# Hybrid SSD/attention/MoE step on one core: expert weight loads issued behind the landing of the unit two places ahead

## Chip, cores and metric

One NeuronCore of a Trainium2 chip, fp32 inputs and outputs. The metric is the device time of one execution in microseconds; lower is better. The median of 3 runs of the kernel before is 777.38 us.

## The reference, cut to what matters

Two layers over 384 tokens of width 1024 (128 context tokens and 256 latent tokens). Each layer has an adaLN-modulated RMSNorm, an attention and state-space mixer, a gated residual, a second modulated norm and a mixture of experts (MoE). The change touches only how the weights of the MoE arrive. What it computes:

```
scores = sigmoid(t @ w_router)                    # 384 tokens x 16 experts
best group of 4 experts per token, then the top 2 experts in it; gates from their scores
hid = silu(t @ w_gate[e]) * (t @ w_up[e]) * gate  # w_gate, w_up: 1024 x 256 per expert
out = sum over e of hid @ w_down[e]               # w_down: 256 x 1024 per expert
```

All 16 experts of both layers are used, so every expert's 3.1 MB is read from HBM once per layer.

## The kernel before, in words

**Units.** All large weights arrive in units of 2 MiB (2.10 MB), each made of two DMAs of 1024 KB, issued by SP. `ORDER` lists the 84 units u = 0 to 83 in the order of issue: those of the conditioning, the input projection, the output projection and, from `MOE_AT[l]` = 22 and 60 on, 24 MoE units per layer. A MoE unit is either the gate and up weights of one expert (k = 0 or 1 of a pair) or the down weights of a pair of experts (k = 2). In this document "place j" is MoE unit j of a layer, j = 0 to 23.

**Slots.** A ring in SBUF has six slots (`SLOTS`), and within the MoE two more lie over an arena that is then free (`EXTRAS`). `SLOT[u]` is the slot of a unit and `EARLIER[u]` the unit that held it; SP waits in L585 until PE has made the last product with that one (`used`, on `s_gu` or `s_dn`). Places 6 and 7 are the first ones in the two extra slots; they have no earlier holder and wait instead for the hidden state to be updated and stored (L587 to L592).

**Landing.** A DMA adds 16 to `landed[u % LANDED]`, eight semaphores in turn, so unit u has landed when its semaphore reaches 32 * (u // 8 + 1). PE waits for exactly this before its first product with a unit (L1804, `arrived`). SP itself waits for no landing of a weight.

**Order of the loads.** Experts are numbered by how many tokens chose them. Experts 0 to 2 are fixed; the others are known only when DVE has ranked them, so SP waits in L580 for `s_order` before place 5 and reads each later expert's number from a register. Place 4 (`SPLIT`) holds the down weights of experts 2 and 3: the half of expert 2 is issued in its place, the half of expert 3 only behind place 5, when expert 3 is known. Behind the MoE loads of layer 0, SP waits for the gathered results (L603) before it issues the input weights of layer 1.

**Blocks.** The tokens of the experts are packed into ten blocks (`BLOCKS`) of 128 rows. For block b, PE makes the gate and up products (L2329, from `gate_up`), ACT and DVE make the hidden rows, PE turns them (L2336), turns the gathered rows of block b + 2 (L2320) and makes the down products of block b (L2344). Place 21 is the gate and up unit of the last expert (its loads go into the arena) and serves the last block, block 9; places 22 and 23 are the last down units.

**The other queues.** POOL gathers the rows of blocks 1 to 9 from HBM (L797, 512 KB each) and, at the end of the MoE, the results of every token (L804, six of 512 KB). ACT stores the results of blocks 0 to 6 to HBM (L1089, 512 KB per block); those of the last three blocks stay in SBUF, and PE adds them by products with a selection (L2390). Every load of a weight is issued in `load` (L534) on SP's queue, q1 in the profile; q0 is POOL's and q10 is ACT's.

Of the kernel before, what the change touches and what calls it, by code (L numbers as in the profile page):

```python
# [40 lines left out]
SLOTS, EXTRAS, LANDED = 6, (6, 7), 8  # L41
# [12 lines left out]
IN_AT, OUT_AT, MOE_AT = [], [], []  # L54
# [137 lines left out]
def hybrid_step(nc, x_prompt, x_sample, cache_k, cache_v, state_ssm, c, c_ctx, norm1_w, norm2_w,  # L192
# [9 lines left out]
    with ctx:  # L202
# [3 lines left out]
        def sem(name):  # L206
            return ctx.enter_context(nc.semaphore(name))
# [157 lines left out]
        landed = [sem(f"landed{i}") for i in range(LANDED)]  # L365
# [58 lines left out]
        def slot(u):  # L424
            return ring[:, SLOT[u], :].rearrange("p (k n) -> p k n", k=KT)

        def unit_at(s):

            return extras[EXTRAS.index(s)] if s in EXTRAS else ring[:, s, :]
# [65 lines left out]
        def overflow(eng, l, step, start=None, stop=None, end=None, more=None):  # L495

            if more is None:
                more = rounds_of(eng, l)
            before = done_rounds.get((id(eng), l - 1), 0)
            with eng.If(more > 0):  # L500
                with eng.Fori(0, more) as r:
                    if start:
                        start(before + r)
                    with eng.Fori(0, E) as e:
                        step(e, before * E + r * E + e)
                    if stop:
                        stop(before + r)
                if end:
                    end(before * E + more * E)
            done_rounds[id(eng), l] = before + more  # L510
# [4 lines left out]
        @block.sync  # L515
        def _(sp):
            def used(u):

                kind, n = ORDER[u]
                if kind == "ada":  # L520
                    return s_ada, n + 1
                if kind == "in":
                    l, j = divmod(n, IN_U)
                    return ((s_q, NT * (l + 1)), (s_xbc, XM * l + 2), (s_xbc, XM * (l + 1)), (s_z, NT * (l + 1)))[j]
                if kind == "out":
                    l, j = divmod(n, OUT_U)
                    return s_o, 2 * NT * l + 5 + j
                l, j = divmod(n, MOE_U)
                pair, k = MOE_UNITS[j]
                return (s_gu, NB * l + GU_BLOCK[2 * pair + k] + 1) if k < 2 else (s_dn, NB * l + DN_BLOCK[pair] + 1)  # L530

            def load(s, parts):
                for dst, src in parts:
                    sp.dma_start(dst, src).then_inc(landed[s], 16)  # L534

            def columns(u, w):
                v = w.rearrange("(k p) n -> p k n", p=P)
                if EARLIER[u] is not None:
                    sp.wait_ge(*used(EARLIER[u]))
                load(u % LANDED, [(slot(u)[:, 4 * i:4 * i + 4, :], v[:, 4 * i:4 * i + 4, :]) for i in range(2)])  # L540

            def ada_unit(u, n):

                l, c = n // ADA_U, ADA_COL[n] % ADA_U
                columns(u, w_ada[l, :, c * 512:(c + 1) * 512])

            def following(u):
                kind, n = ORDER[u]
                if kind == "ada":
                    return ada_unit(u, n)  # L550
                w, units = {"in": (w_in, IN_U), "out": (w_out, OUT_U)}[kind]
                columns(u, w[n // units, :, n % units * 512:(n % units + 1) * 512])

            def gate_up_unit(l, e, u):

                load(u % LANDED, [(unit_at(SLOT[u])[:, i * KT * F:(i + 1) * KT * F], by_row(w[l, e]))
                                  for i, w in enumerate((w_gate, w_up))])

            def down_half(l, e, i, u):

                load(u % LANDED, [(unit_at(SLOT[u])[:, i * 2 * DM:(i + 1) * 2 * DM],
                                   w_down[l, e].rearrange("(p f) n -> p (f n)", f=2))])


            for dst, src in ((prm_rows[32:40, :], c_ctx.rearrange("(k p) -> k p", p=P)),
                             (prm_rows[40:48, :], rows(c)),
                             (prm_rows[108:120, :], rows(conv_b))):
                sp.dma_start(dst, src).then_inc(s_rows, 16)
            u = 0
            for l in range(DEPTH):  # L570
                while u < MOE_AT[l]:
                    if u == 0:
                        sp.dma_start(x[:, 0, :], x_prompt[0]).then_inc(s_x, 16)
                        sp.dma_start(x[:, 1:3, :], x_sample[0].rearrange("(t p) d -> p t d", p=P)).then_inc(s_x, 16)
                    following(u)
                    u += 1
                expert = {x: x for x in range(FIXED)}
                for pair, k in MOE_UNITS:
                    if (pair, k) == (SPLIT[0], 1):
                        sp.wait_ge(s_order, l + 1)  # L580
                    if k < 2 and RANK_OF[2 * pair + k] is not None:
                        r = RANK_OF[2 * pair + k]
                        expert[2 * pair + k] = sp.value_load(order[0:1, r:r + 1], min_val=FIXED, max_val=E - 1)
                    if EARLIER[u] is not None:
                        sp.wait_ge(*used(EARLIER[u]))  # L585
                    else:
                        sp.wait_ge(s_x1, 2 * NT * (l + 1))  # L587
                        if SLOT[u] == EXTRAS[0]:
                            sp.wait_ge(s_bt, 6 * (l + 1))
                        else:  # L590
                            sp.wait_ge(s_h, 16 * NT * (l + 1))
                            sp.wait_ge(s_tx, NB * l + 1)  # L592
                    if k < 2:
                        gate_up_unit(l, expert[2 * pair + k], u)
                    else:
                        for i in range(1 if (pair, k) == SPLIT else 2):
                            down_half(l, expert[2 * pair + i], i, u)
                    if (pair, k) == (SPLIT[0], 1):
                        down_half(l, expert[2 * pair + 1], 1, MOE_AT[l] + UNIT_AT[SPLIT])
                    u += 1  # L600
                if l + 1 < DEPTH:

                    sp.wait_ge(combined[NT - 1], 32 * (l + 1))  # L603
                    while u <= IN_AT[l + 1][-1]:
                        following(u)
                        u += 1

                sp.wait_ge(s_dn, NB * (l + 1))

                def again(e, q):  # L610
                    sp.wait_ge(o_dn, q + 1)
                    for i, w in enumerate((w_gate, w_up)):
                        sp.dma_start(ring[:, OVER_GU, i * KT * F:(i + 1) * KT * F], by_row(w[l, e])
                                     ).then_inc(o_w, 16)
                    sp.dma_start(ring[:, OVER_DN, 0:2 * DM],
                                 w_down[l, e].rearrange("(p f) n -> p (f n)", f=2)).then_inc(o_w, 16)

                def all_used(steps):
                    sp.wait_ge(o_dn, steps + 1)
                    sp.sem_inc(o_pass, 1)  # L620

                overflow(sp, l, again, end=all_used)
            for t in range(NT):
                sp.wait_ge(s_y_out, t + 1)
                dst = y_prompt[0] if t == 0 else y_sample[0, (t - 1) * P:t * P, :]
                sp.dma_start(dst, xn[:, t, :]).then_inc(s_yst, 16)
            sp.wait_ge(s_yst, 16 * NT)
            sp.wait_ge(s_out, 16 * STORES * DEPTH)
# [1854 lines left out]
```

## Time and profile before

| | us |
|---|---|
| median of 3 runs | 777.38 |
| lowest and highest run | 775.66, 777.53 |
| the profiled execution, its own time | 776.23 |
| its span (first to last instruction) | 774.5 |
| PE busy | 724.9 (94%) |
| DVE busy | 324.9 (42%) |
| ACT busy | 213.1 (28%) |
| POOL busy | 138.2 (18%) |
| moved by DMA | 209.33 MB, mean 270 GB/s |
| of it on SP's queue | 179.33 MB |

All times below are microseconds from the start of the span. PE is TensorE, DVE is VectorE, ACT is ScalarE, POOL is GpSimd, SP is SyncE. A name with q behind it (SPq) is the engine's issuing of DMAs. The chain of waits is followed back from the last instruction to what released each piece of work. A row of the timeline or the chain gives start, duration and what ran; a bracket gives the idle time before it and what ended it. PEclk is the granted TensorE clock as a share of 2.4 GHz. The MoE of layer 0 lies at about 250 to 385 us, that of layer 1 at about 618 to 765 us.

### The profile page before, as it was taken

The page shows a single profiled execution, that of the slowest core. Times are in us where ns is not written, and L with a number is a line of the kernel's source. Part 1 is how long each engine was busy: PE and PEld are TensorE (multiplying, and loading weights), DVE is VectorE, ACT ScalarE, POOL GpSimd, SP SyncE. Part 2 cuts the span into 40 slices and gives each one's busy share as a digit, 9 for nine tenths or more (in the row PEclk, how much of TensorE's full clock was granted, in tenths as well). Part 3 has the DMA queues.
Part 4 walks back from the last instruction along what each step waited for, and adds up shares of the span by engine and source line. Part 5 has one row for each costly group of instructions (what it writes and reads, how often), then busy time and mean ns, then how long its engine had stood idle before and what let it go on. Part 6 is the DMA issues. An engine that isn't in the chain of part 4 may idle for free.

```text
span 774.5 us, 10382 instructions
## 1 busy us (share of the span) xinstructions
PE 724.9 (94%) x3940; PEld 354.9 (46%) x3940; DVE 324.9 (42%) x877; ACT 213.1 (28%) x486; POOL 138.2 (18%) x232
## 2 busy tenths in 40 slices
PE   3999998999999999998999999889999899999994
PEld 1447553446445534433344755334544653443331
DVE  2022625637635553312362252473763555231137
ACT  2220145845024101011212024574502310110131
POOL 4056032220010101101112503322001011010202
PEclk9999999999999999999999999999999999999998
DMA  8997335989309899999896233578720389999962
GB/s 319 387 355 263 110 115 212 331 315 364 110 3 337 325 382 391 423 421 423 311 388 230 98 108 116 178 258 306 264 110 4 133 324 390 412 422 423 421 246 82
DMA packets 65639, 209.33 MB, mean 270 GB/s; under 512 B 7736, under 2 KB 8608, under 8 KB 53299
## 3 DMA queue, kind: packets, MB, share of 16 engines
q1 hardware_dynamic: 52744, 179.33, 60.2%
q10 hardware_dynamic: 7723, 16.65, 5.7%
q0 software_dynamic: 5120, 12.66, 4.5%
q8 instruction: 32, 0.52, 0.3%
q14 instruction: 20, 0.16, 0.1%
HBM read 199.92 MB, written 12.88 MB: 275 GB/s over the span
## 4 chain that ended last, share of the span: by engine, by line
PE 75%; DMA 9%; DVE 5%; ACT 4%; SPq 3%; issue 2%; POOL 1%; ACTq 1%; POOLq 0%; DVEq 0%
PE bank L2329 14%; PE bank L2213 11%; PE bank L1955 8%; PE bank L2344 7%; PE bank L2012 5%; PE bank L1900 4%; PE bank L1824 4%; DMA arena<-in_w_up_dram 3%; PE bank L1941 3%; SPq L534 2%; PE bank L2390 2%; DMA ring<-in_w_ada_dram 2%; PE bank L2320 2%; PE bank L2057 2%; DMA arena<-y_exp,y_idx 2%
## 5 line engine op out<-in xcount | busy, mean ns | idle before, releaser
L2329 PE MATMUL bank<-ring,work 128*32 128x512 f32 (+1 forms) x640 | 116.0, 597 | 4.4 <-DMA arena<-in_w_up_dram 3.7
L2329 PEld LDWEIGHTS bank<-ring,work 128*32 128x32 f32 (+1 forms) x640 | 33.7, 121 | 78.1 <-issue 75.0
L2344 PE MATMUL bank<-ring,xs_tok 128*64 128x512 f32 (+2 forms) x320 | 65.7, 597 | 1.5 <-DVE xs_tok L1665 1.0
L1665 DVE COPY xs_tok<-bank 128x256 f32<-128x256 f32 x20 | 8.5, 425 | 138.3 <-PE bank L2336 138.3
L1955 PE MATMUL bank<-arena,ring 128*128 128x384 f32 x192 | 62.2, 486 | 0.0
L2329 PE MATMUL bank<-arena,work 128*64 128x512 f32 (+1 forms) x128 | 58.6, 612 | 0.0
L1824 PE MATMUL bank<-ring,cpad 128*32 128x512 f32 x384 | 50.8, 621 | 7.2 <-DMA ring<-in_w_ada_dram 5.7
L797 POOL DMA_INDIRECT gather_at<-h_rows,idx x18 | 18.2, 1011 | 176.6 <-PE bank L2320 121.2
L1955 PEld LDWEIGHTS bank<-arena,ring 128*128 128x128 f32 x192 | 36.5, 190 | 25.0
L1076 ACT ACTIVATE xs_tok<-bank 128x256 f32<-128x256 f32 x20 | 7.7, 384 | 132.0 <-PE bank L2329 132.0
L2213 PE MATMUL bank<-ring,arena 128*128 128x512 f32 x96 | 43.6, 597 | 0.0
L2213 PE MATMUL bank<-ring,xs_tok 128*128 128x512 f32 x96 | 43.2, 592 | 0.0
L1900 PE MATMUL bank<-ring,arena 128*128 128x512 f32 x96 | 42.8, 597 | 0.4 <-ACT arena L887 0.4
L2012 PE MATMUL bank<-ring,arena 128*128 128x512 f32 x96 | 42.3, 593 | 0.0
L1083 ACT ACTIVATE qkv<-bank 128x512 f32<-128x512 f32 x36 | 19.5, 595 | 74.6 <-PE bank L2344 74.6
L2344 PEld LDWEIGHTS bank<-ring,xs_tok 128*64 128x64 f32 (+2 forms) x320 | 20.5, 131 | 35.0 <-issue 31.4
L1548 DVE COPY work<-bank 128x512 f32<-128x512 f32 x38 | 24.6, 687 | 18.2 <-PE bank L2320 14.5
L1256 DVE SCALAR_TENSOR_TENSOR conv<-arena,prm,conv 128x388 f32<-128x388 f32 x48 | 29.9, 623 | 1.7
L1305 DVE CUSTOM_DVE_ANT_0 arena<-bank,amask 128x384 f32<-128x384 f32 (+1 forms) x48 | 20.1, 466 | 23.9 <-PE bank L2029 23.6
L2213 PEld LDWEIGHTS bank<-ring,xs_tok 128*128 128x128 f32 x96 | 18.2, 190 | 23.0 <-issue 23.0
L2329 PEld LDWEIGHTS bank<-arena,work 128*64 128x64 f32 (+1 forms) x128 | 20.6, 166 | 16.7 <-issue 16.7
L1900 PEld LDWEIGHTS bank<-ring,arena 128*128 128x128 f32 x96 | 17.7, 190 | 22.6 <-issue 20.4
(381 smaller groups left out, 1085.6 us busy)
## 6 DMA issues: line engine op xcount, KB each, us to landing
ring<-in_w_ada_dram SPq DMA_DIRECT2D x48, 1024.0 KB
ring<-in_w_down_dram SPq DMA_DIRECT2D x28, 1024.0 KB
ring<-in_w_gate_dram SPq DMA_DIRECT2D x24, 1024.0 KB
ring<-in_w_up_dram SPq DMA_DIRECT2D x24, 1024.0 KB
ring<-in_w_in_dram SPq DMA_DIRECT2D x16, 1024.0 KB
ring<-in_w_out_dram SPq DMA_DIRECT2D x8, 1024.0 KB
arena<-in_w_gate_dram SPq DMA_DIRECT2D x8, 1024.0 KB
arena<-in_w_up_dram SPq DMA_DIRECT2D x8, 1024.0 KB
```

Of the source, the lines that this page charges most:

```text
L1083: act.activation(y_buf(e)[:, hf * 512:(hf + 1) * 512], bank[5 + hf][:, :], ACT.Copy).then_inc(s_yc, 1)
L1256: ins = dve.scalar_tensor_tensor(out=conv[:, m, :], in0=xpd[:, m, k:k + CONVW], scalar=tap(k), in1=conv[:, m, :], op0=ALU.mult, op1=ALU.add)
L1305: dve.tensor_tensor_reduce(out=probs(t, h), in0=bank[SCORE_BANK[i // 2 % 2][i % 2]][:, 0:nk], in1=amask[:, m0:m0 + nk // P, :].rearrange(" ...
L1548: dve.tensor_copy(xgT[:, b, hf * 512:(hf + 1) * 512], bank[3 + hf][:, :]).then_inc(s_xgc, 1)
L1824: last = mm(bank_of(i)[ADA_TILE * q:ADA_TILE * (q + 1), :], cpad[:, c:c + ADA_TILE], slot(ADA_AT[j])[:, kt, :], start=j == a and kt < ADA_ ...
L1900: last = mm(bank[t][:, :], tok(kt, t), slot(u[0])[:, kt, :], start=kt == 0, stop=kt == KT - 1)
L1941: last = mm(bank[3 + t][:, 0:256], tok(kt, t), slot(u[1])[:, kt, 0:256], start=kt == 0, stop=kt == KT - 1)
L1955: last = mm(bank[(6 + m) % 8][:, 0:3 * P], slot(v)[:, kt, col:col + P], hT[:, kt, :], start=kt == 0, stop=kt == KT - 1)
L2012: last = mm(bank[4 + t][:, :], tok(kt, t), slot(u[3])[:, kt, :], start=kt == 0, stop=kt == KT - 1)
L2213: last = mm(bank[2 * t + hf][:, :], mixed[:, t, kt * P:(kt + 1) * P] if kt < 4 else xs_tok[:, t, (kt - 4) * P:(kt - 3) * P], slot(u + hf)[ ...
L2329: last = mm(bank[b][at:at + n, :].rearrange("p (i f) -> p i f", i=2), rows_T[:, kt * P + at:kt * P + at + n], gate_up_of(s)[:, kt, :, :], ...
L2344: last = mm(bank[5 + hf][at:at + n, :], hidT[:, b, f * P + at:f * P + at + n], w[:, f, hf * 512:(hf + 1) * 512], start=f == 0, stop=f == 1)
```

## The change

Before the DMAs of a MoE unit at place 6 or later are issued, SP now also waits until the unit two places ahead of it has landed. The wait stands behind the wait for the slot. Places 0 to 5, and the units outside the MoE, are issued as before.

```diff
@@ def load(s, parts) ... @@
                 for dst, src in parts:
                     sp.dma_start(dst, src).then_inc(landed[s], 16)
 
+            def landed_first(u):
+
+                sp.wait_ge(landed[u % LANDED], 32 * (u // LANDED + 1))
+
             def columns(u, w):
...
                             sp.wait_ge(s_h, 16 * NT * (l + 1))
                             sp.wait_ge(s_tx, NB * l + 1)
+                    if u >= MOE_AT[l] + SLOTS:
+                        landed_first(u - 2)
                     if k < 2:
                         gate_up_unit(l, expert[2 * pair + k], u)
                     else:
```

## Rows read from the trace of the kernel before

**Rows 1.** The page's 40 slices of 19.4 us: GB/s moved

```profile
GB/s 319 387 355 263 110 115 212 331 315 364 110 3 337 325 382 391 423 421 423 311 388 230 98 108 116 178 258 306 264 110 4 133 324 390 412 422 423 421 246 82
```

**Rows 2.** Windows; from:to, length, five engines' busy us, PEclk, DMA share, GB/s

```profile
287.00:291.00 4.00, 4.00 (x34) 1.80 (x28) 2.14 (x8) 0.38 (x1) 0.00 (x0) 1.00 0.69 229
320.00:330.00 10.00, 10.00 (x80) 4.26 (x74) 4.72 (x17) 0.96 (x3) 0.99 (x1) 1.00 1.02 424
367.02:371.30 4.28, 4.28 (x12) 1.56 (x14) 0.00 (x0) 0.00 (x0) 2.97 (x3) 0.60 1.00 410
653.00:658.00 5.00, 5.00 (x42) 2.13 (x36) 3.10 (x11) 0.38 (x1) 0.69 (x1) 1.00 0.89 317
732.40:737.00 4.60, 4.59 (x22) 1.93 (x24) 0.00 (x0) 0.00 (x0) 3.38 (x5) 1.00 1.01 417
```

**Rows 3.** The chain of waits: start, us, what

```profile
256.91 10.25 DMA gather_at<-h_rows,idx
...
341.85 25.03 DMA arena<-in_w_up_dram
...
367.02 8.78 PE bank L2329 x32
...
707.48 7.02 PE bank L2329 x32
...
736.71 12.85 DMA arena<-y_exp,y_idx
```

**Rows 4.** The timeline of PE, the last row of DVE

```profile
267.21 1.09 PE L2320 MATMUL bank<-ident,gather_at 128*128 128x128 f32 x8 [0.47 <-DMA gather_at<-h_rows,idx]
...
367.02 0.61 PE L2329 MATMUL bank<-ring,work 128*64 128x512 f32 x1 [2.26 <-DMA arena<-in_w_up_dram]
...
732.41 0.61 PE L2329 MATMUL bank<-ring,work 128*64 128x512 f32 x1 [1.40 <-DMA arena<-in_w_up_dram]
...
745.77 3.65 PE L2344 MATMUL bank<-ring,xs_tok 128*64 128x512 f32 x16 [0.50 <-DMA ring<-in_w_down_dram]
...
762.33 1.88 PE L2390 MATMUL bank<-work,qT 128*128 128x512 f32 x4
...
765.11 1.28 DVE L1757 TENSOR_TENSOR arena<-bank,conv 128x512 f32<-128x512 f32 x2
```

**Rows 5.** Who waited for whom, PE: us in total, times, longest

```profile
PE bank L2329 <- DMA arena<-in_w_up_dram: 3.7, 2, 2.3
```

**Rows 6.** SP's DMA queue from 341 to 367 us: packets, MB, share

```profile
q1 hardware_dynamic: 1288, 9.38, 86.1%
```

**Rows 7.** The timeline of SP's issues

```profile
255.15 0.36 SPq L534 DMA_DIRECT2D ring<-in_w_gate_dram  x1
...
257.30 0.34 SPq L534 DMA_DIRECT2D arena<-in_w_gate_dram  x1
...
289.18 0.33 SPq L534 DMA_DIRECT2D ring<-in_w_gate_dram  x1
...
341.42 0.33 SPq L534 DMA_DIRECT2D arena<-in_w_gate_dram  x1
...
622.48 0.34 SPq L534 DMA_DIRECT2D ring<-in_w_gate_dram  x1
```

**Rows 8.** Transfers of 231.3:235.3, 255:268 and 622:635, the latter in 40 slices

```profile
DMA packets 126, 1.03 MB, mean 258 GB/s; under 512 B 0, under 2 KB 0, under 8 KB 0
...
GB/s 0 0 0 202 101 151 302 403 403 403 403 403 403 429 454 429 403 429 429 416 404 416 466 454 378 391 441 429 429 429 429 378 403 454 429 378 403 429 429 454
...
GB/s 0 0 0 50 202 0 176 252 479 403 403 403 429 429 403 403 429 403 429 429 429 479 353 466 429 378 479 441 454 366 416 441 391 454 403 403 429 403 403 429
```

**Rows 9.** SP's DMA queue from 742 to 743 and 745 to 745.8 us

```profile
q1 hardware_dynamic: 18, 0.13, 31.5%
...
q1 hardware_dynamic: 1, 0.00, 0.1%
```

**Rows 10.** POOL's gathers of rows (L797) in layer 0

```profile
DMA to landing us min/median/max: 9.0/9.1/9.6
```

## The prediction, made before the changed kernel was built or run

> **What bounds the kernel now.** I read the 40 slices first, to see where TensorE and the DMA engines are full together. A slice is 19.4 us. In the slices from 290 to 368 us and from 639 to 736 us the transfers run at 390 to 423 GB/s, and no slice of the kernel is above 423 [rows 1]. These are the two mixture-of-experts stages. A window inside one shows PE busy 10.00 of 10.00 us and the DMA share at 1.02, at 424 GB/s [rows 2]. So in this stage a transfer slot that is lost is lost, unless a dry stretch comes later that can take it up.
>
> The chain of waits shows what ends the stage. In layer 0 the last step from a transfer into PE is the load of place 21, the last gate and up weights: its second half is issued at 341.85 us and lands 25.03 us later. The block behind it takes 8.78 us where the same 32 products take 7.02 us in a block that was not held up [rows 3]. The timeline of PE gives the pauses themselves: 2.26 us before 367.02 and 1.40 us before 732.41, both for place 21 of its layer, and 0.50 us before 745.77 for the last down weights; the products of one block wait for a gate and up load nowhere else (3.7 us, 2 times in all) [rows 4, 5]. The windows give the clock's part: after the pause in layer 0 the granted clock is 0.60 in the mean over 4.28 us, so part of it at 1.2 GHz; behind the shorter one in layer 1 it stays at 1.00, 2.4 GHz [rows 2]. So weight landings set PE at the end of both stages, and everything before that has cover.
>
> **The change, part by part.** It adds 36 waits on SP, 18 per layer, from place 6 on: unit u is issued only when u-2 has landed. No byte, load or product is added, and nothing runs on another engine. Queued behind a waiting SP are only the other weight loads; gathers go out from POOL, result stores from ACT. Behind the MoE loads of layer 0 stand the input weights of layer 1, which wait for the gathered results anyway.
>
> *A wait that is already fulfilled.* It is one more small step of a queue whose issues last 0.3 to 0.4 us each, with long pauses between them [rows 7]; I cost it at nothing. The cover is the weights already in flight; with the queue empty a wait would cost its own length, far below 0.3 us.
>
> *The steady stretch.* Between 341 and 367 us SP's queue moved 9.38 MB in 26 us, 361 GB/s [rows 6]. A unit is 2.10 MB, hence 5.8 us. The load issued at 341.42 [rows 7] landed at 366.88, 25.5 us later, so it had more than three units ahead of it. Under the change it is issued when the unit two ahead has landed, 366.88 - 2 x 5.8 = 355.3 us: 14 us later, yet still one unit (5.8 us) ahead of its turn. What a start needs is the time from issue to flow. I take it from three starts into an empty queue [rows 8]. From 231.3 to 235.3 us 1.03 MB moved where 424 GB/s would have moved 1.70: 0.67 MB short, 1.6 us. In the eight slices of 0.325 us from 255.0 the rates add to 1159 where full ones would add to 3392, short by 1.7 us, 0.15 of it before the issue at 255.15 [rows 7]; the same sum from 622.0 (680) is short by 2.1 us, 0.5 us of which lies before the issue at 622.48 [rows 7]. So 1.6 us. Behind it comes the lag from the last bytes to the landing: the last down weights release PE at 745.77, and from 745.0 on their queue moved nothing [rows 4, 9]: 0.8 us. The two together, 2.4 us, are less than 5.8. In the steady stretch the cost is 0; the upper end is below, as a rival.
>
> *The first wait, at place 6.* Place 4 is the split one: its first half goes out early, its second half after place 5, once the order of the experts is known. So "two places ahead" is here the last thing in the queue: loads at 255.15 and behind them that half, and today right after it place 6 at 257.30 [rows 7]. With the change this one waits until the queue is empty: three halves of 1.05 MB and two gathers of 0.52 MB, 4.2 MB at 424 GB/s, are 9.9 us, so to about 255.15 + 1.6 + 9.9 = 266.7 us. It costs 1.6 + 0.8 = 2.4 us of transfer time in each layer. Unevenness of the 16 engines adds to it: at 742 to 743 us the queue is already down to a share of 31.5% while it drains, so some engines run out some 2 to 3 us before the last [rows 9]. An engine idle on the average for 1 us more makes 3.4 us; the low end is 1.6 us, the start alone. I take 2.4.
>
> *What takes it up.* PE doesn't need place 6 soon (it serves block 3, and the only pauses for gate and up weights are those before block 9 [rows 4, 5]), so the loss counts only as a later stream. The stream of before runs dry once more, because a slot comes free late (the load issued at 289.18 [rows 7]): 287 to 291 us at 229 of 424 GB/s is a gap of 4 x (1 - 0.54) = 1.8 us; in layer 1, 653 to 658 us at 317 GB/s is 1.3 us [rows 2]. A delay up to there closes that gap. Net: layer 0 2.4 - 1.8 = 0.6 us (ends 0 and 1.6), layer 1 2.4 - 1.3 = 1.1 us (ends 0.3 and 2.1).
>
> *What a later stream costs.* Layer 0: place 21 lands 0.6 us later and PE, already waiting for it, starts 0.6 us later; the half clock is paid now as before. The chain from there on is PE's: +0.6 us. Layer 1: the pause grows from 1.40 to 2.5 us, more than the 2.26 us that came before the half clock in layer 0. I add that loss, 8.78 - 7.02 = 1.76 us [rows 3], to PE: +1.1 + 1.8 = +2.9, less the 0.50 us it now waits for the last weights: +2.4. At the end DVE takes up some of it: PE's last products end at 764.21 and DVE starts on them at 765.11 [rows 4], 0.9 us of slack. But the last gathered results (736.71 + 12.85 us in the chain [rows 3]) share the same full engines and shift by about 1.1. The larger of 2.4 - 0.9 = 1.5 and 1.1 counts: +1.5 us. The ends are 0.3 (no half clock) and 3.2 us.
>
> *A gain.* At 267.16 the first gather ends and PE had waited 0.47 us for it [rows 3, 4]; with place 6 held back, SP's queue thins out behind it. At most -0.5 us; I take -0.1, since the 3 MB issued before are still ahead.
>
> *Longer waits in passing.* The blocks in the middle never waited for weights [rows 5]. Still, I put +0.6 us for the 34 other waits together (a few starts that come a few tenths late): low 0, high 5.
>
> **Sum:** 0.6 + 1.5 - 0.1 + 0.6 = +2.6 us. The profiled execution took 776.23 us (span 774.5, 1.7 around it): 778.8. The median of the runs lies 1.15 us above the profiled one: 780.0.
>
> The Trainium skill, "DMA: Bandwidth & Descriptors", section "Anatomy of one DMA", gives a fixed cost of about 2.0 us for setup and completion of a transfer on GpSimd's path. By it, an estimate from that page, the bubble would be 2.0 instead of 2.4 us and the sum 0.8 us less. The rows above are of SP's own queue, so they decide.
>
> **The rivals.**
> (A) *It makes nothing.* The bubble is swallowed by the dry stretch and nothing else moves: -1 to +1.5 us. For it: in layer 0 the dry stretch is nearly as large. Against it: in layer 1 it is half. 778.
>
> (B) *Faster: engines in step, shorter queues.* If the 424 GB/s is one shared limit and not sixteen, holding the leading engines back hands their share to the last one, whose landing releases PE. The lead is some 2 to 3 us [rows 9], so a landing comes 1 to 1.5 us earlier; in layer 0 the pause falls to 1 us, at which layer 1 kept its clock: 1.2 + 1.8, and about 1 us in layer 1, less bubbles of 1.7: about -2.3, 775. Against it: the gathers take 9.0 to 9.6 us under full load, all within 0.6 us of each other [rows 10], which looks like a fixed price and not like a queue that stands behind SP's.
> The Trainium skill, same page, section "Queues, rings and completion order", says that each DMA engine goes round-robin over the queue rows with work. By that rule the depth of SP's queue is nothing to the others. The spread of the gathers agrees with it.
>
> (C) *Slower by more: the steady stretch starves.* At a landing only 5.8 us of weights are left, less on a leading engine. The margin is 5.8 - 2.4 = 3.4 us; from where an engine leads by more, it stands idle each time. If the leads are due to chance and move from engine to engine, the loss isn't made good. At 0.4 us for each of about 12 units per layer it is 5 us of stream, per layer, all on the path from place 21: with the above +10, 787. For it: leads of 2 to 3 us are near 3.4.
>
> (D) *The waits hold nothing back*, since slots come free later than u-2 lands. Against it: the load issued at 341.42 landed 25.5 us later. It would give 777.4, and counts with (A).
>
> **How the numbers follow.** Chances: forecast 0.50 (+1.3 to +5 us), A with D 0.25, B 0.13, C 0.12. A measurement of this kernel can tell about 0.3%, 2.3 us, from no change. Of the forecast 0.34 lies above that and 0.16 below; C is slower; a tenth of B stays within. Slower 0.46, same 0.43, faster 0.11. The range runs from 776 (all but B's better half) to 784, 0.8% above the median; what is left out is C's larger part and B's.
>
> **What would show it.** Right: place 6 issued at about 267 in layer 0 and, by the same sum from 622.48, at about 634 in layer 1, with a hole of 2 to 3 us in the DMA slices there; the hole before 291 closed; the pause before block 9 in layer 0 at 2.5 to 3.5 us; a clock below 1.00 after the one in layer 1; the issue of place 21 near 356 us instead of 341.4; DMA share at 1.01 still. Wrong: place 21 of layer 0 landing before 366.9; a share below 0.98 in the steady stretch (C); gathers that land in under 8 us (B).

## The result and the profile after

| | before | changed |
|---|---|---|
| median, us | 777.38 | 783.98 |
| lowest and highest of 7 runs | 775.66, 777.53 | 782.53, 788.22 |
| the profiled execution, its own time | 776.23 | 788.22 |
| its span | 774.5 | 786.5 |
| ratio to before, 95% interval | | 1.0100 (1.0084 to 1.0115) |

The change makes the kernel slower: the medians differ by 6.6 us (0.8%), and the ratio, which is not simply that of the two medians, gives 1.0%, 7.8 us. A second measurement, against other runs of before, gave 1.0108 (1.0092 to 1.0124), 8.4 us. The forecast was slower by 2.6 us, at 780.0; the median, 783.98, lies just inside the edge of the stated range, but the rise is 2.5 to 3 times the forecast one.

The profiled execution is the slowest of the seven, so its steps are sized against its own +12.0 us of span; a second profile of the same kernel follows below. First the page's 40 slices of the changed kernel:

```profile
PEclk9999999999999999999999999999999999999898
DMA  8996336998217799999895233678531289999951
GB/s 320 387 356 241 108 113 226 343 326 311 107 63 286 305 393 399 409 414 421 337 386 184 79 107 114 213 243 321 214 108 53 82 343 403 400 414 416 409 213 80
```

Where the fullest slices of before held 421 to 423 GB/s in both MoE stages [rows 1], there are now 399 to 421 and 400 to 416. The windows of the changed kernel (from:to, length, five engines' busy us, PEclk, DMA share, GB/s) show where it begins, and what came after the pauses:

```profile
255.00:273.00 18.00, 17.12 (x145) 8.90 (x146) 8.62 (x29) 2.26 (x3) 3.17 (x3) 1.00 0.74 284
273.00:303.00 30.00, 30.00 (x200) 12.01 (x200) 12.72 (x61) 3.33 (x7) 1.98 (x2) 1.00 0.99 388
303.00:357.00 54.00, 52.40 (x304) 20.52 (x298) 14.18 (x43) 6.96 (x14) 3.96 (x4) 1.00 1.01 413
...
371.94:378.00 6.06, 6.06 (x18) 2.08 (x20) 0.00 (x0) 0.00 (x0) 0.00 (x0) 0.61 1.01 414
...
742.85:749.00 6.15, 6.15 (x16) 2.04 (x18) 0.00 (x0) 0.00 (x0) 1.85 (x2) 0.52 1.02 422
```

The same three stretches of the kernel before, for comparison:

```profile
255.00:273.00 18.00, 17.15 (x144) 8.80 (x144) 8.43 (x29) 2.26 (x3) 3.17 (x3) 1.00 0.95 381
273.00:303.00 30.00, 30.00 (x200) 12.03 (x200) 12.93 (x61) 3.33 (x7) 2.18 (x3) 1.00 0.96 375
303.00:357.00 54.00, 54.00 (x310) 21.04 (x304) 13.96 (x43) 6.96 (x14) 3.75 (x4) 1.00 1.02 423
```

Against before, the first stretch lost 18 x (381 - 284) = 1.75 MB, 4.1 us at 424 GB/s. The second won back 30 x (388 - 375) = 0.39 MB, 0.9 us, and the third lost 54 x (423 - 413) = 0.54 MB, 1.3 us. So there are two losses: a hole at the start and a slightly thinner steady stretch. The dry stretch from 287 to 291 us did close, as forecast: 408 GB/s there instead of 229.

The hole of layer 1 is smaller. The same 18 us, laid from 0.15 us before the issue of place 5, in the kernel before and in the changed one:

```profile
622.33:640.33 18.00, 17.61 (x144) 8.48 (x144) 8.21 (x24) 2.26 (x3) 3.16 (x3) 1.00 0.94 380
...
628.06:646.06 18.00, 17.55 (x142) 8.44 (x142) 8.22 (x24) 2.26 (x3) 3.16 (x3) 1.00 0.82 311
```

That is 18 x (380 - 311) = 1.24 MB, 2.9 us.

Inside the hole of layer 0, the slices of 0.2 us from 262 to 270 us of the changed kernel:

```profile
GB/s 512 307 533 389 430 410 471 328 512 492 246 451 328 82 246 82 0 0 0 0 0 0 0 0 1 164 164 143 225 307 205 82 225 143 41 143 410 287 287 369
```

The timeline of SP's issues (compare [rows 7]):

```profile
256.27 0.38 SPq L534 DMA_DIRECT2D ring<-in_w_down_dram  x1
267.46 0.34 SPq L534 DMA_DIRECT2D arena<-in_w_gate_dram  x1
268.32 0.34 SPq L534 DMA_DIRECT2D arena<-in_w_up_dram  x1
...
360.54 0.33 SPq L534 DMA_DIRECT2D arena<-in_w_gate_dram  x1
...
639.28 0.33 SPq L534 DMA_DIRECT2D arena<-in_w_gate_dram  x1
```

Place 6 goes out at 267.46 us instead of 257.30. The rates are full until 264.4, at zero from 265.2 to 266.8, and full again only from 269.2. Between the last bytes and SP's next issue lie 2.2 us (the landing itself comes at 267.22), and 1.7 us more between that issue and full flow. What moves from 267.0 us on, before SP's issue, is a gather of POOL.

In layer 1 the same wait ended sooner. The slices of 0.1 us from 637 to 641 us of the changed kernel:

```profile
GB/s 615 164 328 328 246 328 410 328 123 205 164 41 164 41 82 41 0 0 0 0 0 0 1 0 246 246 123 41 205 123 369 328 451 287 164 205 123 164 123 41
```

The rates thin out from 637.8, the last bytes move before 638.6, and place 6 goes out at 639.28: 0.7 us. Every traced kernel in which place 6 waits for place 4 shows this difference (the change, e1, e3, e4, e5, e9, e10 and e12): from the last bytes of SP's own queue to the issue about 2.5 us in layer 0 and about 0.9 us in layer 1. Why layer 0 waits longer, no run shows.

The end of the stage, in the chain of waits of the changed kernel (start, us, what), to be read beside [rows 3]:

```profile
360.97 10.84 DMA arena<-in_w_up_dram
...
371.94 9.44 PE bank L2335 x32
...
742.85 10.01 PE bank L2335 x32
```

And the pauses, in the timeline of PE:

```profile
354.88 7.09 PE L2335 MATMUL bank<-ring,work 128*64 128x512 f32 x32 [1.60 <-DMA ring<-in_w_up_dram]
...
371.94 1.09 PE L2335 MATMUL bank<-ring,work 128*64 128x512 f32 x1 [5.14 <-DMA arena<-in_w_up_dram]
...
725.95 7.09 PE L2335 MATMUL bank<-ring,work 128*64 128x512 f32 x32 [0.82 <-DMA ring<-in_w_up_dram]
...
742.85 1.09 PE L2335 MATMUL bank<-ring,work 128*64 128x512 f32 x1 [4.99 <-DMA arena<-in_w_up_dram]
```

Layer 0: the pause before block 9 grew from 2.26 to 5.14 us, one of 1.60 before block 8 is new, and the block itself took 9.44 us instead of 8.78: +5.1 us. Layer 1: 1.40 became 4.99, 0.82 is new, the block took 10.01 instead of 7.0, and the pause of 0.50 for the last down weights is gone: +6.9 us, of which DVE at the end takes up some. By the order of the experts (628.21 instead of 622.48 us at place 5) the shift was 5.7 us; at the end it is 12.0. PE's other work is untouched.

The bytes until the landing of place 21 show one thing more. POOL issues its gathers of the results at about 364 us in either kernel. In the kernel before none of their bytes had moved when place 21 landed at 366.88; in the changed kernel its queue moved this between 357 and 371.8 us:

```profile
q0 software_dynamic: 220, 0.61, 10.6%
```

So a late place 21 shares the engines with them. From 255 us on, 1.75 - 0.39 + 0.54 = 1.90 MB of transfers were lost (4.5 us), these 0.61 MB went ahead (1.4 us), and SP's queue had moved 37.39 instead of 37.86 MB by the landing, 0.47 MB less of the weights behind place 21 (-1.1 us): 4.8 of the 4.9 us by which the block starts later (371.94 against 367.02).

### The profile page after: what moved, and what is told of

It is laid out like the page before. It is cut to its first block, busy times and chain, and to the rows that moved or that the text cites. A ratio compares the mean times of both kernels' runs of the same rounds, so it can differ in the third digit from the quotient of the medians.

```text
span 786.5 us, 10416 instructions
## 1 busy us (share of the span) xinstructions
PE 728.4 (93%) x3940; PEld 355.4 (45%) x3940; DVE 325.2 (41%) x877; ACT 212.8 (27%) x486; POOL 135.9 (17%) x232
## 4 chain that ended last, share of the span: by engine, by line
PE 55%; DMA 29%; DVE 5%; SPq 4%; ACT 3%; issue 2%; ACTq 1%; POOL 0%; POOLq 0%; DVEq 0%
PE bank L2219 11%; DMA arena<-in_w_up_dram 9%; DMA ring<-in_w_up_dram 9%; PE bank L1961 8%; PE bank L2018 5%; DMA ring<-in_w_down_dram 5%; PE bank L1906 4%; PE bank L1830 4%; PE bank L2396 4%; SPq L534 4%; DMA arena<-in_w_down_dram 3%; PE bank L1947 3%; PE bank L2335 2%; DMA ring<-in_w_ada_dram 2%; PE bank L2350 2%
## 5 line engine op out<-in xcount | busy, mean ns | idle before, releaser
L2335 PE MATMUL bank<-ring,work 128*32 128x512 f32 (+1 forms) x640 | 119.8, 604 | 13.3 <-DMA arena<-in_w_up_dram 10.1
L2335 PEld LDWEIGHTS bank<-ring,work 128*32 128x32 f32 (+1 forms) x640 | 35.3, 122 | 89.9 <-issue 86.8
L2335 PE MATMUL bank<-arena,work 128*64 128x512 f32 (+1 forms) x128 | 62.1, 642 | 0.0
```

The costliest lines, as they stand in the source:

```text
L2335: last = mm(bank[b][at:at + n, :].rearrange("p (i f) -> p i f", i=2), rows_T[:, kt * P + at:kt * P + at + n], gate_up_of(s)[:, kt, :, :], ...
```

## The experiments

All medians stand against runs of the kernel before on the same chip, in groups: 776.40 us for e1 to e4, 776.12 for e5 to e8, 776.21 for e9 to e11 and 776.13 for e12 and e13. A cost in us below is the ratio less 1, times that median.

### e1, e2: the first wait alone, the others alone

```diff
-                    if u >= MOE_AT[l] + SLOTS:
+                    if u == MOE_AT[l] + SLOTS:     # e1; e2: if u > MOE_AT[l] + SLOTS:
                         landed_first(u - 2)
```

> The only wait left is that of place 6, behind the landing of place 4 (whose second half is the last load in the queue). First theory (the emptied queue at place 6 is the cause): some 3.5 to 4 us of transfers are lost in each layer, 1.6 us of it is taken up at 287 to 291 us in layer 0 and 0.7 us in layer 1; with the longer pauses of PE and the half clock behind them this gives +4 to +5 us of the +6.6, and place 21 of layer 0 lands 2 to 3 us later than in the kernel before. Second theory (the many waits of the steady stretch are the cause): under +2 us, place 21 within 1 us of the kernel before.

> All waits of the change but that of place 6, so the queue never runs empty at place 6. First theory: +1 to +2.5 us, what the steady stretch lost in the trace (1.3 us of transfers between 303 and 357 us in layer 0, about as much in layer 1), with the DMA share at 1.01 and 416 to 424 GB/s there. Second theory: +4 to +6 us. If the sum of this and of the kernel with place 6 alone is well above 6.6 us, the two hide behind each other; if it is well below, they need each other.

e1: 781.67 us, ratio 1.0063 (1.0049 to 1.0077), +4.9 us. e2: 777.03 us, 1.0010 (0.9998 to 1.0022), +0.8 us. One wait per layer makes most of the loss, the other 34 almost none by themselves. The sum, 5.7 us, is less than the whole (7.8 and 8.4 us in the two measurements of the change). The windows of e1:

```profile
255.00:273.00 18.00, 17.20 (x144) 8.81 (x144) 8.44 (x29) 2.27 (x3) 3.17 (x3) 1.00 0.77 283
273.00:303.00 30.00, 30.00 (x200) 12.03 (x200) 12.97 (x61) 3.33 (x7) 2.24 (x3) 1.00 1.01 414
303.00:357.00 54.00, 53.56 (x308) 21.00 (x302) 13.91 (x43) 6.97 (x14) 3.71 (x4) 1.00 1.02 422
```

The hole is the same as in the change (283 GB/s). But behind it the queue is full without a gap, at 414 GB/s, and wins back 30 x (414 - 375) = 1.2 MB, and the steady stretch is back at 422. What the waits at the later places add is to be seen beside the second profile of the change, below.

### e3: the change once more

> The change itself once more. Its profiled execution took 788.22 us, while the other six took 782.5 to 785.0. Theory of the clock: the difference between executions is how much half clock falls behind the two pauses; this profile should again show pauses before block 9 of about 5 us in both layers, and a total of 783 to 785 us where the half clock is shorter. Rival: the transfers differ from execution to execution, then the landing of place 21 moves by some us against the start of its stage.

784.58 us (781.84 to 786.45). Its profiled execution took 781.84 us, the fastest of its five. The timeline of PE there:

```profile
369.29 1.08 PE L2335 MATMUL bank<-ring,work 128*64 128x512 f32 x1 [4.67 <-DMA arena<-in_w_up_dram]
...
737.67 0.61 PE L2335 MATMUL bank<-ring,work 128*64 128x512 f32 x1 [3.58 <-DMA arena<-in_w_up_dram]
```

The chain of waits gives the two blocks:

```profile
369.29 9.22 PE bank L2335 x32
...
737.67 8.78 PE bank L2335 x32
```

Pause and landing move too: place 21 starts PE at 369.29 instead of 371.94 us, with no pause before block 8 in either layer. So both the rival and the theory have a part: of the 6.4 us between the two profiled executions 4.3 us are pauses and 1.5 us are the two blocks (9.22 and 8.78 us against 9.44 and 10.01). The transfers of one and the same kernel differ by some 2.5 us at place 21 between executions. The windows of this execution:

```profile
273.00:303.00 30.00, 30.00 (x204) 11.99 (x204) 13.16 (x62) 3.33 (x7) 2.42 (x3) 1.00 1.01 412
303.00:357.00 54.00, 54.00 (x310) 21.23 (x304) 13.72 (x43) 6.97 (x14) 3.53 (x4) 1.00 1.01 413
```

Behind the same hole (287 GB/s from 255 to 273 us) this execution wins back 30 x (412 - 375) = 1.1 MB, 2.6 us, as e1 does. The 0.9 us of the first profile is therefore no rule of the change. What both executions share is the thinner steady stretch: 413 GB/s, where e1 has 422 and the kernel before 423.

### e4, e5, e6: PE's clock kept

Small products of PE into a free bank are put ahead of the wait for block 9: 16 and 8 of them in the change (e4, e5), 3 in the kernel before (e6).

```diff
                 for b in range(NB):
+                    if b + 1 == NB - 1:
+                        clock_kept(2, 8)     # e4: 16; e6: 3, in the kernel before
                     if b + 1 < NB:
```

> The change, with 16 small products of PE ahead of its wait for block 9, some 3.9 us inside the pause of 5 us, so that PE's clock has no reason to fall; transfers untouched. Theory of the clock (the half clock behind the pauses is a part of the loss): block 9's gate and up products take 7.0 us instead of 9.4 and 10.0, and the time falls by 2 to 4 us against the change, to 780 to 782. Rival (the pauses alone cost, the clock is taken up later): within 1 us of the change.

> The change with 8 small products of PE ahead of block 9's wait. Sixteen of them ran 7.1 us (0.44 us each) and were longer than the pause of 4.7 to 5.1 us; eight run 3.6 us and lie inside it. Theory of the clock: block 9's gate and up products take 7.0 us instead of 8.8 to 10.0 in both layers and the time falls by 2 to 3.5 us against the change. Rival: what the clock costs is taken up behind block 9 (by the wait for the last down weights, by DVE at the end), and it stays within 1 us of the change.

> The kernel before with 3 such products, 1.3 us, ahead of block 9's wait, inside its pauses of 2.3 and 1.4 us; no waits added. Theory of the clock: the idle time left is 1 us, the half clock of 3.4 us in layer 0 goes, block 9 takes 7.0 us instead of 8.8: -1 to -1.8 us. But the last down weights of layer 0 landed only 1.1 us before PE came to them, so 0.7 us of it may turn into a pause for them. Rival: the half clock does not fall in most executions, then no change (within 0.5 us).

e4: 786.08 us, 1.0118 (1.0100 to 1.0136). It answers another question than the one I asked, since I had sized the filler wrongly. Its timeline of PE:

```profile
366.27 7.17 PE L1858 MATMUL bank<-amask,ident 128*128 128x256 f32 x32
373.38 0.64 PE L2335 MATMUL bank<-ring,work 128*64 128x512 f32 x1
```

Sixteen ran for 7.17 us, longer than the pause, and PE came late by itself. But block 9 took the 7.02 us of a block that was not held up, in both layers, so the filler does keep the clock; in the chain of waits of e4:

```profile
373.44 7.02 PE bank L2335 x32
...
745.32 7.02 PE bank L2335 x32
```

e5: 782.66 us, 1.0072 (1.0051 to 1.0093), +5.6 us. Against the 1.0108 of the change without the filler that is 2.8 us less, as the theory had it, though the two intervals just overlap, and by the medians, each against its own runs of before (+6.5 and +8.2 us), it is only 1.6 us. In e5 another wait comes up, for the last down weights:

```profile
383.07 3.65 PE L2350 MATMUL bank<-ring,xs_tok 128*64 128x512 f32 x16 [1.85 <-DMA ring<-in_w_down_dram]
...
752.37 5.35 PE L2350 MATMUL bank<-ring,xs_tok 128*64 128x512 f32 x16 [2.28 <-DMA ring<-in_w_down_dram]
```

The second of these took 5.35 us for the 16 products that take 3.65 us in the first: behind the pause of 2.28 us the half clock falls here instead, as the granted clock of that stretch (0.68) shows:

```profile
752.37:757.70 5.33, 5.33 (x17) 1.78 (x17) 3.56 (x3) 2.29 (x2) 0.00 (x0) 0.68 0.05 20
```

So a part of what the clock gives back is taken by the next late load. e6: 775.82 us, 0.9997 (0.9985 to 1.0009): in the kernel before the filler gains nothing that can be measured. No version here beats the kernel before.

### e8, e11: the same place, but the queue not emptied

```diff
-                    if u >= MOE_AT[l] + SLOTS:
-                        landed_first(u - 2)
+                    if u == MOE_AT[l] + SLOTS:      # e8: this wait alone
+                        landed_first(u - 1)
+                    if u >= MOE_AT[l] + SLOTS:      # e11: all 36, place 6 behind place 5
+                        landed_first(u - (1 if u == MOE_AT[l] + SLOTS else 2))
```

> One wait per layer only, that of place 6, but behind the landing of place 5 instead of place 4. Behind place 5 the second half of place 4 (1.05 MB) is still in the queue, 2.5 to 4 us of transfers. First theory (it is the emptied queue that costs, not a wait at this place): the hole shrinks to 0 to 1.5 us, which the dry stretch behind it takes up: within 1 us of the kernel before. Rival (holding back the loads at this place costs by itself, whatever is in flight): +3 to +5 us, as with the wait for place 4.

> All 36 waits of the change, but place 6 waits for the landing of place 5 instead of place 4, so that one half load is still in flight. If the emptied queue is what both parts need: within 0.3% of the kernel before, +0 to +1.5 us. Rival (any delay at place 6 takes away the cover of the later waits): +2.5 to +4 us.

e8: 776.24 us, 0.9995 (0.9983 to 1.0007), no cost that can be measured. Its place 6 was issued at 263.05 us, also held back, but with half a unit still in flight:

```profile
255.00:273.00 18.00, 16.66 (x142) 8.77 (x142) 8.34 (x29) 2.26 (x3) 3.17 (x3) 1.00 0.91 359
273.00:303.00 30.00, 30.00 (x196) 12.06 (x196) 12.50 (x62) 3.33 (x7) 1.98 (x2) 1.00 0.97 381
```

The first stretch has 359 GB/s where the change had 284. e11, with all 36 waits, one of them moved by one place: 777.56 us, 1.0016 (1.0003 to 1.0029), +1.2 us instead of +8.4. It is the emptied queue that costs, not that SP waits. (Its place 6 went out at 262.68 us, some 5 us earlier than in the change; a delay as long as that of the change with the queue still full was not tried.)

### e7: the price of a start, many times

```diff
                     if u >= MOE_AT[l] + SLOTS:
-                        landed_first(u - 2)
+                        landed_first(u - 1)
```

> The suspected cost made many: from place 6 on each unit waits for the landing of the unit directly before it, so nearly each of 18 units per layer starts into an empty queue. First theory: each such start costs 3 to 4 us of transfers (2 us from the last bytes to the landing, 1.5 to 2 us from the issue to full flow), so a unit takes some 9 to 10 us instead of 6, and the stream of a layer gets 45 to 65 us longer: +90 to +130 us in all. Rival (a start costs 2.4 us, as I put it in the prediction): +55 to +75 us.

864.54 us, 1.1133 (1.1103 to 1.1162), +87.9 us: below the 90 of the first theory, above the 75 of the rival. SP's issues there give the price:

```profile
365.41 0.33 SPq L534 DMA_DIRECT2D ring<-in_w_gate_dram  x1
...
372.81 0.33 SPq L534 DMA_DIRECT2D ring<-in_w_gate_dram  x1
...
381.32 0.81 SPq L534 DMA_DIRECT2D ring<-in_w_down_dram  x2
388.71 0.33 SPq L534 DMA_DIRECT2D ring<-in_w_gate_dram  x1
...
396.09 0.33 SPq L534 DMA_DIRECT2D arena<-in_w_gate_dram  x1
```

Three of these units took 7.4 us from issue to issue; 2.10 MB at 424 GB/s are 4.95, so a start out of an empty queue costs 2.4 us. In two of the three, from 365.41 and from 381.32 us, no other queue moved anything. The end of the latter, from 386 to 390 us in slices of 0.1 us:

```profile
GB/s 328 410 573 328 328 573 410 328 492 492 164 573 573 164 573 573 164 410 164 0 0 0 0 0 0 0 0 0 0 0 0 0 0 0 0 0 246 246 164 0
```

The last bytes move before 387.9, the next issue comes at 388.71: 0.8 us, and 0.7 and 0.9 us at the issues of 381.32 and 372.81. That is the price of the prediction, in its lag of 0.8 us too. The hole at place 6 is larger than a clean start, by 0.5 us in layer 1 and by 1.7 us in layer 0.

### e9, e10: which waits add to the first

```diff
-                    if u >= MOE_AT[l] + SLOTS:
+                    if MOE_AT[l] + SLOTS <= u < MOE_AT[l] + 12:                    # e9
+                    if u == MOE_AT[l] + SLOTS or u >= MOE_AT[l] + 12:              # e10
```

> Place 6 alone cost 4.9 us, the other waits alone 0.8 us, all together 8.2 us against the same runs of before: the rest needs both. First theory (the dry stretches at 287 to 291 and 653 to 658 us can hide one loss only: alone, the waits of places 7 to 11 are hidden there, but behind the hole of place 6 they are not): waits at places 6 to 11 give nearly the full +7 to +8 us. Second theory (with a late stream the limit of two units in flight binds in the steady stretch, at places 12 to 23): +5 us, as with place 6 alone.

> Waits at place 6 and at places 12 to 23, none at 7 to 11. First theory (one dry stretch, two losses before it): +5 to +5.8 us, place 6 plus at most the 0.8 us of the rest. Second theory (the limit binds in the steady stretch once the stream is late): +7 to +8 us, with 400 to 415 GB/s between 303 and 357 us instead of 421 to 424.

e9: 783.27 us, 1.0092 (1.0078 to 1.0106). e10: 783.30 us, 1.0093 (1.0078 to 1.0109). Both cost some +7.2 us. Each theory foretold its own kernel and missed the other's, so neither holds alone: on top of place 6 (+4.9) either half of the other waits adds about 2.2 us, and both halves together little more (+7.8 to +8.4 in the two measurements of the change). The windows of layer 0, one execution each, fit: from 273 to 303 us e9 has 396 GB/s and e10 417, from 303 to 357 us e9 has 422 and e10 414, where e1 has 414 and 422.

### e12, e13: do the costs add once the clock is kept?

```diff
                 for b in range(NB):
+                    if b + 1 == NB - 1:
+                        clock_kept(2, 8)     # e12: in e1; e13: clock_kept(2, 4) in e2
                     if b + 1 < NB:
```

> The wait of place 6 alone, with 8 small products of PE (3.6 us) in the pause before block 9, which was 4.7 and 3.6 us. Theory: the clock makes the costs more than additive, since a half clock follows only behind a longer pause. Then with the clock kept, place 6 alone costs +2.5 to +4 us instead of +4.9, and this plus the cost of the other waits with the clock kept (the next kernel) is within 1.5 us of the +5.6 that the whole change costs with the clock kept. Rival (the transfers themselves need both): place 6 alone with the clock kept +1 to +2.5 us, the other waits +0.5, and the sum stays 2.5 us or more below 5.6.

> All waits but that of place 6, with 4 small products (1.8 us) in the pause before block 9, which was 2.1 and 3.3 us. Theory of the clock: +0.5 to +2 us, as without them (+0.8) or a little less, since a half clock followed in some executions only. Rival: +0.5 us at most, and the sum with place 6 alone stays 2.5 us or more below 5.6.

e12: 781.04 us, 1.0062 (1.0044 to 1.0081), +4.8 us. e13: 777.10 us, 1.0016 (1.0002 to 1.0031), +1.2 us. Their sum is 6.0 us, and the whole change with the clock kept (e5) cost 5.6: with the clock kept the costs add, as the theory of the clock has it; without, 4.9 and 0.8 stood against 8.4. But the same theory wanted place 6 alone to get cheaper by 1 us or more, and it didn't. In e12 PE waited 1.83 and 0.61 us for the last down weights, which can hide such a gain. So that the half clock makes the costs more than additive fits the sums, and isn't shown.

## Why the prediction was wrong, point by point

**The mechanism was right.** Place 6 was to go out at about 267 and 634 us (plus the shift of its layer); it went out at 267.46 and 639.28, the latter 11.07 us behind the issue of place 5, where the sum gave 11.5. The hole was there, the dry stretch behind it closed, the pauses of block 9 grew, the clock fell in layer 1 too, and place 21 went out at 360.54 us, still one unit ahead of its turn. The sizes were not those foretold: the pause in layer 0 was to be 2.5 to 3.5 us and was 5.14 (4.67 in e3). e1 shows that this one wait makes 4.9 us of the loss by itself, and e8 and e11 that it does so because it empties the queue.

**The step that failed first: the cost of the wait at place 6.** For this wait alone the sum had 0.6 + 1.5 - 0.1 = 2.0 us; e1 measured 4.9. The term that was mis-sized is the hole in layer 0. I took 2.4 us (1.6 for the start, 0.8 for the lag from the last bytes to the landing) and gave 3.4 as the upper end. Measured against before it was 4.1 us in layer 0 (e1 alone: 18 x (381 - 283) = 1.76 MB, the same), but 2.9 us in layer 1, inside the ends, and a clean start costs the 2.4 us (e7). The lag differs between the layers by about as much: in layer 0 the issue came 2.2 us behind the last bytes, in layer 1 0.7 us, in e7 0.7 to 0.9 us. So the 0.8 us, read off the end of layer 1, was right for layer 1 and for e7 and missed layer 0; why it is longer there stays open. Smaller parts are that the engines drained over some 0.8 us in layer 0 and some 0.8 us in layer 1, which I had left out as "unevenness", and that between the issues of the two halves of place 6 lie 0.86 us (0.42 us elsewhere), as they did in the kernel before, where other loads covered it.

The Trainium skill, "DMA: Bandwidth & Descriptors", section "Anatomy of one DMA", puts most of its fixed 2 us behind the last byte, as the receipt of the write, on GpSimd's path. The 2.2 us of layer 0, on SP's queue, look like that, but the 0.7 us of layer 1 and the 0.7 to 0.9 us of e7 on the same queue do not, so the page's figure is no rule for these loads.

**The path from the stream to PE.** I also put the shift of PE equal to what the stream lost. In layer 0 of the changed kernel the results' gathers, 0.61 MB of them, moved ahead of the late place 21, 1.4 us that the sum didn't have (0.31 MB in e1, 0.21 MB in e3, none in the kernel before).

**What takes it up.** I gave the dry stretch as 1.8 us; with place 6 alone 1.2 MB were won back, 2.8 us, more than I thought, because the whole stretch from 273 to 303 us ran fuller. With all waits it was 0.9 us in one execution and 2.6 us in the other (e3), so this term was too small rather than too large and doesn't explain the loss.

**The steady stretch** was costed at 0 with +0.6 us for all other waits. By themselves they cost 0.8 us (e2), which is that. Behind the hole they cost 2.9 or 3.5 us (7.8 or 8.4 less 4.9). This is the second step that failed: I had added the terms, and they don't add. Rival C's mechanism (the stretch starves) is there in small: 413 GB/s instead of 423 in both profiles of the change, a DMA share still at 1.01, not the 10 us of the rival. Why a late stream makes these waits cost more than alone is not shown.

**The clock.** I counted one half clock more, 1.76 us, in layer 1. In e3 it was just that (8.78 us against 7.02), and 0.4 us more in layer 0; in the first profiled execution the block took 3.0 us longer in layer 1 and 0.7 us longer in layer 0. In the mean keeping the clock is worth 1.6 to 2.8 us in all (e5), with the reserve of overlapping intervals.

**Put together:** instead of 0.6 and 1.5 us, the profiled execution has 5.1 us of PE time in layer 0 and 6.9 in layer 1; it is the slowest, and the median execution lost 6.6 us, a little over half of that. Rivals A, B and D fall: what the dry stretch took up was not enough, the kernel did not get faster, and SP did wait.

**A side argument that was wrong.** Against rival B I said that gathers landing in 9.0 to 9.6 us [rows 10] look like a fixed price and not like a queue behind SP's. The one issued while SP's queue was empty landed twice as fast. POOL's gathers of rows in the changed kernel's layer 0, and in both layers of e7:

```profile
DMA to landing us min/median/max: 4.1/8.8/10.0
```

```profile
DMA to landing us min/median/max: 4.2/5.3/10.4
```

Gathers under 8 us were on my list of what would speak for rival B, and some came, without B's gain. The conclusion stood (of the gathers of rows PE waits for none but the first), the reason didn't. The gathers do pay for SP's loads; only how deep SP's queue is changes little, as long as it is never empty: with two units in flight (e2) they took 8.7 to 9.7 us.

## What to carry to other kernels

Before a load waits for another load's landing, look up what else will be in flight at that moment: here 34 of 36 such waits were almost free by themselves, and one per layer, whose "two places ahead" was in fact the last thing issued, cost 4.9 us for the two layers. A split or reordered load makes an index distance mean something else than a queue distance. In a stage where transfers and PE are both full, price an emptied queue by the trace of an emptied queue, drain and landing included, at the place in question, and don't simply add the price of a further limit: here it cost more behind the emptied queue than alone.

## What the runs showed of the hardware that I had not expected

From the last bytes to the issue that waited for them took 2.2 us at place 6 of layer 0, 0.7 us at place 6 of layer 1 and 0.7 to 0.9 us in e7; a clean start from empty costs 2.4 us per 2.10 MB unit (e7). A gather of 512 KB took 4.1 us when it was issued beside an empty SP queue and 9.0 to 9.6 us beside a full one. A pause of TensorE of 2.28 us was followed by a granted clock of 0.68 (e5, layer 1), one of 2.06 us by 1.00 (e2, layer 0). The transfers of one and the same kernel differ by 2.5 us at place 21 between two executions (369.29 and 371.94 us), while e11, with all waits but no emptied queue, shows no delay there (366.23 us against the 367.02 of the kernel before).
